# The last tile of a down projection in two halves, and the following norm and query tiles begun on the first half

## The reference, cut to what matters

```
# layer 0, end: the same weights for latents and context
x = x + g2  * swiglu(h)  @ ffn_w_down[0]
y = y + cg2 * swiglu(hc) @ ffn_w_down[0]
# layer 1, beginning
h  = rms(x, norm1_g[1]) * (1 + sc1)  + sh1
hc = rms(y, norm1_g[1]) * (1 + csc1) + csh1
q        = rms(h @ w_in[:, :1024]) per head      # latents only
k, v     = h  @ w_in[:, 1024:]                   # latents
kc, vc   = hc @ w_in[:, 1024:]                   # context
```

## Time and profile before

| | |
|---|---|
| median of the runs before | 2153.16 us (lowest 2150.04 us) |
| the profiled execution | 2153.89 us |
| its span | 2152.1 us |
| mean granted clock of TensorE | 0.989 of full speed |
| PE busy | 2074.6 us (96% of the span) |
| DVE busy | 1499.1 us (70%) |
| ACT busy | 975.7 us (45%) |

### The profile page before, as it was taken

The page is one execution under the profiler, slowest core; times in us unless marked ns, Lnnn a source line. Parts: engine busy times, 40 slices in busy tenths (PEclk is TensorE's granted clock), DMA queues, the critical chain, the costliest instruction groups (busy, mean ns, idle before and its releaser), DMA issues.

```text
span 2152.1 us, 34724 instructions
## 1 busy us (share of the span) xinstructions
PE 2074.6 (96%) x12633; PEld 1772.4 (82%) x12633; DVE 1499.1 (70%) x2685; ACT 975.7 (45%) x1545; POOL 321.9 (15%) x340
## 2 busy tenths in 40 slices
PE   7998999999989988999999999999999999999998
PEld 3755778888878757999999988999988888888887
DVE  4535578894247745665597867997986677777776
ACT  3426332222234355444469535446743444444444
POOL 0114000000004021000000006787830000000000
PEclk8999999999999999999999999999999999999999
DMA  8352345694226303455554534551256655555553
GB/s 290 118 179 88 108 146 190 209 327 143 98 79 177 100 9 102 149 180 186 174 176 162 201 128 144 171 183 54 69 166 216 198 192 186 192 188 188 190 188 117
DMA packets 92896, 342.18 MB, mean 159 GB/s; under 512 B 10383, under 2 KB 10399, under 8 KB 92272
## 3 DMA queue, kind: packets, MB, share of 16 engines
q1 hardware_dynamic: 89280, 325.10, 45.0%
q0 software_dynamic: 3504, 15.56, 2.5%
HBM read 339.57 MB, written 1.05 MB: 158 GB/s over the span
## 4 chain that ended last, share of the span: by engine, by line
PE 89%; DVE 4%; ACT 3%; issue 2%; DMA 1%; POOL 0%; SPq 0%; DVEq 0%; ACTq 0%; POOLq 0%
PE banks L1015 20%; PE banks L1455 16%; PE banks L1064 9%; PE banks L1421 7%; PE banks L1333 6%; PE banks L1204 5%; PE banks L1424 3%; PE banks L1382 3%; PE banks L942 2%; PE banks L1366 2%; PE banks L1104 2%; PE banks L1029 2%; PE banks L968 1%; PE banks L1217 1%; PE banks L764 1%
## 5 line engine op out<-in xcount | busy, mean ns | idle before, releaser
L1015 PE MATMUL banks<-act_parts,first_w_parts 128*128 128x512 f32 (+1 forms) x2544 | 464.0, 343 | 3.1 <-DVE ffn_hidden_parts L2050 1.8
L1015 PEld LDWEIGHTS banks<-act_parts,first_w_parts 128*128 128x128 f32 x2544 | 400.4, 190 | 64.0 <-issue 7.3
L1455 PE MATMUL banks<-w_parts,a_parts 128*128 128x512 f32 x1524 | 360.4, 390 | 0.1
L2050 DVE TENSOR_TENSOR first_w_parts<-weight_ring,first_w_parts 128x1024 fp32r<-128x1024 f32 x166 | 206.8, 1248 | 207.0 <-ACT first_w_parts L1635 206.9
L1455 PEld LDWEIGHTS banks<-w_parts,a_parts 128*128 128x128 f32 x1524 | 285.9, 188 | 59.4 <-issue 0.8
L2050 DVE TENSOR_TENSOR w_parts<-weight_ring,w_parts 128x1024 fp32r<-128x1024 f32 x207 | 253.7, 1226 | 74.3 <-ACT w_parts L1635 71.8
L1635 ACT ACTIVATE w_parts<-weight_ring 128x1024 fp32r<-128x1024 f32 x207 | 218.9, 1058 | 184.0 <-PE banks L1421 102.1
L1635 ACT ACTIVATE first_w_parts<-weight_ring 128x1024 fp32r<-128x1024 f32 x166 | 174.8, 1056 | 236.1 <-PE banks L1015 124.1
L1421 PE MATMUL banks<-n_parts,w_parts 128*128 128x512 f32 x632 | 229.4, 397 | 1.3 <-DVE w_parts L2050 1.3
L1064 PE MATMUL banks<-ffn_hidden_parts,first_w_parts 128*128 128x512 f32 (+1 forms) x1056 | 183.4, 336 | 0.0
L1064 PEld LDWEIGHTS banks<-ffn_hidden_parts,first_w_parts 128*128 128x128 f32 x1056 | 162.5, 190 | 20.6
(11 more groups left out here) (315 smaller groups left out, 2903.8 us busy)
## 6 DMA issues: line engine op xcount, KB each, us to landing
weight_ring<-in_stream SPq DMA_DIRECT2D x618, 512.0 KB, 3.3
main_zone<-in_rel_bias POOLq DMA_DIRECT2D x6, 512.0 KB, 11.7
rounded<-in_dft_input POOLq DMA_DIRECT2D x1, 1600.0 KB, 7.5
rounded<-in_dft_inverse POOLq DMA_DIRECT2D x1, 1280.0 KB, 6.1
main_zone<-in_xT POOLq DMA_DIRECT2D x1, 1024.0 KB, 12.6
main_zone<-in_ctxT POOLq DMA_DIRECT2D x1, 1024.0 KB, 17.7
main_zone<-in_c_rows POOLq DMA_DIRECT2D x1, 1024.0 KB, 6.9
tail_zone<-in_rel_bias POOLq DMA_DIRECT2D x2, 512.0 KB, 24.2
```

The costliest lines, as they stand in the source:

```text
L1015: mm = pe.matmul(o[:, 0:w], wb[:, hw, k, :], fin[:, hx, k, 0:w], start=(k == 0 and n == 0), stop=(k == DC - 1 and n == 2))
L1455: mm = pe.matmul(acc[n][:, :], ap_[:, e % 3, ha, (n // 2) * P:(n // 2 + 1) * P], wp[(B + b) % PARTS][:, hw, (n % 2) * 512:(n % 2 + 1) * 51 ...
L2050: return dve.tensor_tensor(o, a, b, op)
```

## The change

The last tile of the first down projection is computed as a latent half (256 columns) and then a context half, each with its own bank, so the projection has 9 tiles to count and every later tile takes the next bank. The latent half's square sums, root, reciprocal and spreading (into bank 5) are interleaved with the matmuls of the context half. The context's own root follows, and is spread into bank 3 after `split_first`. The scaling and rounding of the context half are taken out of the norm: they stand on DVE behind the low parts of blocks 3 to 8 (`CONTEXT_LOW`) and on ACT behind the tiles 0 to 5 (`CONTEXT_HIGH`). Tile 8, the first one with context columns, waits for all of them. POOL's bias loads wait for the context's norm as well.

```diff
-TILES = [..., ("ffn_d0", 8), ("od_in", 16), ...
+TILES = [..., ("ffn_d0", 9), ("od_in", 16), ...
+        CONTEXT_HIGH = {0: (0,), 1: (1,), 2: (2,), 3: (3,), 4: (4, 5), 5: (6, 7)}
+        CONTEXT_LOW = {3: ((0, None),), 4: ((1, 0), (2, 1)), 5: ((3, 2),), 6: ((4, 3),), 7: ((5, 4), (6, 5)), 8: ((7, 6), (None, 7))}
...
+            def down_last():                                   # PE
+                pe.wait_ge(mod_used, len(MODS))
+                for c in range(DC - 2):
+                    add_squares(2, c)
+                o = bank_of(TILE[name] + m)
+                for k in range(FC):
...
+                        mm = pe.matmul(o[:, 0:L], wb[:, hw, b % 8, :], fhid[:, hx, k, 0:L],
...
+                    if k == 11:
+                        add_squares(2, DC - 2)
+                mm.then_inc(tile_ready, 1)
+                o = bank_of(TILE[name] + DC)
+                for k in range(FC):
...
+                        mm = pe.matmul(o[:, L:T], wb[:, hw, b % 8, :], fhid[:, hx, k, L:T],
...
+                    if k == 5:
+                        pe.wait_ge(squares_ready, squared(2, DC - 2) + 1)
+                        add_last_squares((0, 1))
+                    if k == 10:
+                        pe.wait_ge(rstd_ready, 3)
+                        spread_half(0)
...
+                    if k_norm == 2 and k == 5:                  # in split_first
+                        pe.wait_ge(squares_ready, squared(2, DC - 1))
+                        add_last_squares((2, 3))
...
             split_first("od_in", L, 2)
+            pe.wait_ge(rstd_ready, 4)
+            spread_half(1)
             for j in range(2, 16):
+                if j == 8:
+                    pe.wait_ge(normed, DC * nth(2) + DC)
                 split_tile("od_in", j, L if j < 8 else T)
...
+            def norm_latents():                                # ACT
+                evacuated(act, "ffn_d0", DC)
+                act.activation(sq[:, c, 0:L], X[:, c, 0:L], ACT.Square).then_inc(squares_ready, 1)
+                root_half(0)
+                high("od_in", 0)
+                high_half(0, 0)
+                high("od_in", 1)
+                for n in range(1, 5):
+                    high_half(0, n)
+                evacuated(act, "ffn_d0", DC + 1)
+                act.activation(sq[:, c, L:T], X[:, c, L:T], ACT.Square).then_inc(squares_ready, 1)
+                high("od_in", 2, begun=False)
+                for n in range(5, DC):
+                    high_half(0, n)
+                root_half(1)
...
             for j in range(16):
                 project_in(1, "od_in", j, 0)
                 if j >= 2:
                     qk_root(1, j - 2)
+                for c in CONTEXT_HIGH.get(j, ()):
+                    high_half(1, c)
...
+            def norm_latents():                                # DVE
+                last_half(0)
+                turned_half(0)
+                low("od_in", 0)
+                for c in range(DC):
+                    scaled_half(0, c)
+                    if c >= 1:
+                        low_half(0, c - 1)
+                    if c == 1:
+                        low("od_in", 1)
+                    if c == 4:
+                        last_half(1)
+                    if c == 6:
+                        low("od_in", 2)
+                low_half(0, DC - 1)
+                turned_half(1)
...
                         low(name, split)                       # in qk_norm
+                        if l == 1:
+                            for above, below in CONTEXT_LOW.get(split, ()):
+                                if above is not None:
+                                    scaled_half(1, above)
+                                if below is not None:
+                                    low_half(1, below)
...
-            evacuated(pool, "ffn_d0", DC)
-            pool.wait_ge(normed, DC * 3)
+            evacuated(pool, "ffn_d0", DC + 1)
+            pool.wait_ge(normed, DC * nth(2) + DC)
```

More of the change, by code:

```diff
@@ L809, in norm, with add_last_squares, spread_half @@
                     add_squares(k, c)
+            def add_last_squares(strips):
+                d = norms[2]
+                w = T // 4
+                for j in strips:
+                    mm = pe.matmul(bank[6][32 * j:32 * j + 32, 0:w], ones[:, 0:32], d["sq"][:, DC - 1, j * w:(j + 1) * w],
+                                   start=False, stop=True)
+                mm.then_inc(sumsq_ready, 1)
+            def spread_half(s):
+                w = T // 4
+                r = slice(64 * s, 64 * s + 64)
+                for j in (2 * s, 2 * s + 1):
+                    mm = pe.matmul(bank[[5, 3][s]][:, j * w:(j + 1) * w], small("strip")[r, j:j + 1].broadcast_to([64, P]),
+                                   rstd[r, 0:w], start=True, stop=True)
+                mm.then_inc(rstd_spread, 1)
@@ L1677, in ffn @@
                     if l == 0:
-                        if m == DC - 1:
-                            for b in range(PARTS - 1):
-                                high("od_in", b)
-                        square(2, m)
+                        if m < DC - 1:
+                            square(2, m)
                     else:
@@ L2341, in ffn @@
                     if l == 0 and m == DC - 1:
-                        for n in range(PARTS - 1):
-                            low("od_in", n)
+                        return
                     if l == 1 and m == DC - 1:
@@ L2414, in _ @@
             ffn(0, T)
[L2415 removed]
+            norm_latents()
             qk_norm(1)
```

95 lines of the change are left out of this document (70 added, 25 removed).

## The result

The changed kernel took 2159.18 us (median of 20 runs, 2153.34 to 2164.39), and the kernel before 2150.01 beside it (median of 20, lowest 2149.05). One of those 20 took 2582.49 us and is not in the ratio. The ratio is 1.0039, with a 95% interval of 1.0032 to 1.0046: a loss of 8.4 us, 6.9 to 9.9 (the medians differ by 9.2), small but real. It is far inside the 2% that count as no change.

The account below looks back on a forecast made before the run. PE's work plus its waits bound the kernel, with DVE as full as PE in the narrow tiles. From 2153.9: 10.1 gained, 10.0 given back, +0.3 and +2.7 make 2156.8, given as 2157, range 2148 to 2164.

Parts of the forecast that it names:

- The split: Last down tile: 132 matmuls of 256 columns replace 66 of 512, 15.0 us becoming 15.9, +0.9 on PE.
- The latents' norm: During the context half: root, reciprocal and spreading hidden there, spreading ended at 625.7 against 632.1, 6.4 us earlier.
- The ladder: DVE and ACT steps over eight chunks before tile 2: tile 2 begins at 638.3 instead of 648.4, 10.1 us gained.
- The context's share: Narrow tiles before tile 8: moved context steps meet a full DVE, and 10.0 us are given back by tile 8.
- The walk: ACT and DVE queues stepped through tiles 3 to 8: they wait in turn, the stretch taking 30.4 us, not 20.4.
- The round of 3.30 us: Narrow tiles 2 to 8 before the change: time per round, filled by DVE's three operations at 3.32 us.
- Rival 1: Narrow tiles: DVE's work alone is the bound, tile 8 begins between 663.8 and 668, 2149 to 2154 us; chance 0.23.
- The bank: First value blocks: tile 15 now lies in their fourth bank, so they wait for its copy, about +0.3 us.
- POOL's subtractions: Last four wide tiles: subtractions hold DVE operations, price taken as 4 us, +2.7 over the 1.35 of before.
- the landing: POOL's loads, issued at 668.4: landed 22 to 33 us later, so POOL works from 690 to 701 on.
- rival 3: Last wide tiles: four DVE operations held by POOL, plus half clock after waits before tiles 7 and 8; 2162, up to 2166; chance 0.17.
- value blocks that begin after 726: Value blocks: a start this late in the changed profile would mark the forecast wrong and rival 3 right.

Follow-up runs that it names:

- e6: The kernel before with only its last down tile in two passes into one bank, norm and ladder behind both: 1.0002, 2151.35 us.
- e1: The changed kernel with the context's scalings, high parts and low parts in another order on DVE and ACT: ratio to before 1.0002, 2151.86 us.
- e3: The changed kernel with both the other order of the context's share and POOL's subtractions held back: ratio to before 0.9990, 2150.67 us.
- e10: As e3, but the context's low parts spread over blocks 5 to 8 and chunk 5's high part a tile earlier: ratio to before 0.9970, 2143.87 us.
- e11: As e10, with banks 2 and 0 exchanged between the two groups of value blocks: ratio to before 0.9968, 2144.18 us.
- e2: The changed kernel with POOL's four subtractions held back until all of the projection's norms are done: ratio to before 1.0013, 2152.98 us.
- e7: The kernel before with POOL's four subtractions held back until DVE has multiplied the last of the 16 tiles: 0.9980, 2147.50 us.
- e13: The changed kernel unaltered, profiled and timed again beside e10 and e11 on one chip: ratio to before 1.0046, 2159.50 us.
- e4: The kernel before with only POOL's loads issued later, when tile 7 of the 16 is ready: 1.0009, 2152.90 us.
- e9: The kernel of e3 unaltered, one more execution for a third profile: 2146.56 us.
- e12: The kernel of e3 unaltered, timed again beside e10 and e11 on one chip: ratio to before 0.9976, 2144.83 us.

## Why the prediction was right, and where its terms were off

The prediction was 2157 us with a range of 2148 to 2164, and the median is 2159.2. The forecast of no change within 2% was right, and so was the account of where PE waits and for whom. The loss was forecast at 2.9 us and is 8.4. That the time came nearer than that is luck: the execution from which the sum started, 2153.9, lies 3.9 us over the median of the 20 runs of the kernel before (2150.0), and the median that the forecast had, 2153.16, was of three runs only. From 2150.0 the same sum gives 2152.9, just under the lowest of the changed kernel's 20 runs (2153.34).

- *The split: right.* +0.9 forecast, +0.9 in e6.
- *The latents' norm hidden under the context half: right.* PE did not wait ahead of the spreading. It came at offset 14.6 in place of 13.0. Here a count was wrong: a chunk's square sum is four matmuls in the program and eight in the trace, so six chunks are 48 of the 64 and not 24, and took 1.45 us in place of 0.8. The seventh chunk's sum took 0.36 and the two strips 0.34, where the forecast had 0.1 for the strips and nothing for the seventh. The rest are matmuls of the halves, at 0.125 us each in place of 0.120.
- *The ladder: right in kind, 2.5 us too good.* Tile 2 began at offset 28.4; 638.3 is an offset of 25.9. The gain is 7.4 us (28.4 against 35.8) in place of 10.1; 0.2 of the difference is only that the forecast took tile 2 before from the chain. Some 1.6 us are the late spreading, the rest is the spreading itself (0.64 in place of 0.3) and steps of the ladder. Half clock did vanish from it, as forecast.
- *The context's share: right.* The walk gave waits of 2.0 us ahead of tile 4 and of 4.0 ahead of tile 7, each released by ACT's root; the trace has 1.80 and 3.85, and ACT stands 3.60 and 3.47 us for DVE where the walk said so. Ahead of tile 8 it gave 2.9, and the trace has 0.41. What the walk left out is that tile 7 runs at half clock after its wait and takes 2 us longer, which uses up most of the wait of tile 8. So the half clock at tile 7 cost nearly nothing. In all 9.5 us were given back, for 10.0 forecast. With the smaller gain, tile 8 began 2.1 us late and not level. (The round of 3.30 us is that of five of the six rounds; 20.38 / 6 is 3.40, the first being 3.89. DVE, with 3.32 a round, was as full as the forecast says.)
- *Rival 1 (DVE's work alone is the bound): refuted for the order of this change* by e1, in which tile 8 begins 6.7 us earlier with equal work. But its lower bound for DVE's work, 663.8 or offset 51.4, is where tile 8 stands in e1, e3 and e10. That the two agree so closely is partly luck: e1's work began at 29.3 in place of 27.3, with four reciprocals ahead of tile 8 where the forecast counted five.
- *The bank: +0.3 forecast, +0.6 measured* (e10 against e11).
- *POOL's subtractions: the term that was mis-sized.* The price of 4 us for them, and with it the +2.7 over before, is the term of the sum that came out smallest against its measurement. Without collisions the second value block begins at 115.58 (e2) in place of 121.74, and in the kernel before at 112.85 (e7) in place of 114.57: 6.16 against 1.72, so +4.4. The issue (offset 56.9 against 56.0) and the landing of 32 us (in the range of 22 to 33, at its long end) were right; the first subtraction came at offset 89.3, just behind the range of 77.6 to 88.6 (690 to 701). PE's wait of 3.25 us, for a price of 4, was nearly right as well, though the slack was smaller than forecast: DVE was held for 4.4, 1.0 and 4.3 us ahead of tile 15, 9.7 in all, which leaves a lead of 6.5 us where the sum had 7.4 and 1.1 more per tile. What the sum left out is what it put into rival 3 alone, and there for tiles 7 and 8 and at 1.5 us: after that wait, tile 15 runs at half clock for more than half its length, 8.38 us in place of 5.47. That is +2.9. Wait and clock together are 6.2, as e2 shows.

The terms then add up to the stage. Tile 8 is late by 2.1, the bank costs 0.6, POOL 4.4: 7.1, for 7.2 in the table. The timed difference is 8.4 with an interval from 6.9, so that the stage explains it down to about a microsecond (two by the medians).

Rival 3, the slower one, had the right ingredients. Its trigger, a third operation that is held for 4.4 us, was wrong: two such (5.63 and 5.55) and one held for about 1 between them (1.72) were enough, since the second stood directly ahead of the last tile. (A fourth, 1.68 in place of 0.75 at 719.65, came when tile 15 had begun.) The sign that the forecast named for rival 3, value blocks that begin after 726, was missed by 0.04 us (725.96) only because this execution reached the stage 1.6 us earlier: by offsets it is 113.6 and the first value block stands at 115.2. In the wide tiles the case therefore went the way of rival 3, and the forecast's time came so near with the help of the start of its sum.

## What to carry to other kernels

Work that is moved out of a ladder with idle time goes somewhere, and where the engine there is full, the order decides what it costs: write down both queues that wait for each other and move the steps on which one waits until the other has passed its next result on. Ask of each load or background operation whose trigger the change moves where it lands now; here the collisions cost 6.2 us, nearly the 7.4 that the ladder gave. Beside a wait of PE of some 3 us, set a second term for the half clock that may follow it.

## What the runs showed of the hardware that was not expected

- **A wait can cost twice.** Waits of 3.25 to 3.98 us were each followed by a lowered granted clock: 0.50 over the first 4 us of tile 15 (after and e13), 0.53 to 0.54 over tile 7 (after, e2, e13), 0.67 and 0.72 over the first 3 us of the first value block (e1 and e4). The next tile or block took 1.9 to 2.9 us longer (7.32, 7.36, 8.38 and 8.44 for 5.47; 5.19 to 5.38 for 3.14). Some 0.3 of that comes with a wait at full clock too (5.72 to 5.79 for 5.47). At 2.5 us it was a matter of the execution: 5.74 us in e3, 7.37 in e9. Behind single waits of 0.9 to 1.8 us in the narrow and wide tiles the clock stayed up (3.14 to 3.22, and 5.76 to 5.79). Whether the end of the stage moves by it depends on what is waited for next: at tile 15 it did, at tile 7 hardly. The Trainium skill, "TensorE: Matmul & The Clock Gate", section "HAM oscillation — how this bites in real kernels", describes a clock that falls when the array is idle; the rows agree in kind, and the price above is theirs.
- **The landing took as long in either place.** From POOL's first issue to its first subtraction it was 32.9 us in the kernel before, mostly among narrow tiles, and 32.4, 33.4 and 32.0 in the changed kernel, e1 and e4, among wide ones. The forecast had let it fall to 22, since wide tiles draw half as much. But the DMA engines were as full: their share was 1.04 at 244 GB/s (651 to 680 us, before) and 1.00 at 227 GB/s (671 to 700, after). What the landing would take beside much less traffic, no run here shows.
- **A weight part of DVE that meets a subtraction takes 5.54 to 5.64 us in place of 1.22** (six of them in the changed kernel, e1 and e4), while the reciprocal, with one input, ran in its usual 3.34 beside a subtraction (705.79 above). The multiplication of 512 columns beside one took 1.7 to 2.1 in place of 0.75.
- **Same code, a mean clock of 0.992 or 0.988.** The executions of e3 differ by 7 us in this way, and of e12 too (0.992 to 0.993 in its eight, 0.987 to 0.989 in its four). The clock is enough to explain the size: 0.004 of 2145 us is an estimated 8.6 us of full-clock time lost. What makes it was not found.
